# Four reorderings in a two-layer hybrid decoder step: scaled keys, held weight sums, split sample states, modulation panels in pairs

## The reference, cut to what matters

```
mod = silu(c) @ ada_w[l] + ada_b[l]            # 1024 x 9216, nine chunks of 1024
u   = rmsnorm(x) * (1 + sc1) + sh1
x   = x + 0.5 * g1 * swiglu(u, up, down)       # first FFN, 2816 hidden
proj = u @ w_in                                # four branches
y_b = rwkv7(...)                               # recurrence over tokens
merged = sum_i sigmoid(u @ w_gate[i]) * (y_i @ w_branch[i])
x   = x + g2 * (merged @ w_out)
x   = x + 0.5 * g3 * swiglu(u, up, down)       # second FFN
```

```
S = S * w_t + (S @ -kk_t) (kk_t * a_t)^T + v_t k_t^T ;  y_t = S @ r_t
```

## Time and profile before

| | us |
|---|---|
| median of 3 runs | 3047.55 |
| lowest, highest | 3044.19, 3050.33 |
| the profiled execution | 3045.21 |
| its span, first to last instruction | 3043.5 |

### The profile page before, as it was taken

One profiled execution on the slowest core, in us unless ns is written; L12 is line 12 of the kernel. 1 busy time (PEld: TensorE's weight loads), 2 busy tenths in 40 slices (PEclk: granted clock), 3 DMA queues, 4 the chain that ended last, 5 costly groups with the idle time before them and its releaser, 6 DMA issues.

```text
span 3043.5 us, 48463 instructions
## 1 busy us (share of the span) xinstructions
PE 3001.7 (99%) x19566; PEld 2461.5 (81%) x19566; DVE 1428.1 (47%) x3125; ACT 410.6 (13%) x782; POOL 1473.8 (48%) x1527
## 2 busy tenths in 40 slices
PE   8999999999999999999999999999999999999999
PEld 5889888677777878898878898876777778789987
DVE  4446522464344464565244564324544444555642
ACT  2000002202111120000010000022021111200000
POOL 4879530212120338896368894302222113599943
PEclk9999999999999999999999999999999999999999
DMA  6543223541111334222246322334311114122221
GB/s 262 216 165 111 101 99 132 171 139 41 53 54 61 117 115 167 98 84 91 76 173 229 125 84 86 126 122 153 129 59 53 53 60 159 70 84 84 84 87 68
DMA packets 73535, 337.81 MB, mean 111 GB/s; under 512 B 10592, under 2 KB 27744, under 8 KB 40288
## 3 DMA queue, kind: packets, MB, share of 16 engines
q1 hardware_dynamic: 63936, 312.03, 28.8%
q0 software_dynamic: 6816, 18.88, 2.1%
q10 hardware_dynamic: 2560, 3.80, 0.4%
HBM read 326.55 MB, written 6.02 MB: 109 GB/s over the span
## 4 chain that ended last, share of the span: by engine, by line
PE 91%; DVE 3%; POOL 3%; issue 1%; DMA 1%; ACT 1%; SPq 0%; POOLq 0%; DVEq 0%; ACTq 0%
PE ps L1000 90%; DVE ws L2287 1%; DMA y<-w_ada 1%; DVE u L2287 1%; DVE proj L2287 0%; POOL masked_room L901 0%; ACT ws L1966 0%; DVE y L2287 0%; POOL ws L860 0%; DVE masked_room L2287 0%; ACT u L1966 0%; POOL ws L866 0%; POOL ws L864 0%; POOL ws L868 0%; POOL ws L863 0%
## 5 line engine op out<-in xcount | busy, mean ns | idle before, releaser
L2287 DVE TENSOR_TENSOR ws<-ws,ps 128x272 f32<-128x272 f32 (+4 forms) x1650 | 620.2, 401 | 1122.2 <-PE ps L1000 1094.8
L1000 PE MATMUL ps<-u,ring 128*128 128x272 f32 (+1 forms) x4448 | 1040.3, 385 | 6.9 <-ACT u L1966 2.5
L1000 PEld LDWEIGHTS ps<-u,ring 128*128 128x128 f32 x4448 | 802.6, 191 | 187.8 <-issue 22.5
L1000 PE MATMUL ps<-y,ws 128*128 128x272 f32 (+1 forms) x1616 | 343.3, 348 | 0.0
L1000 PEld LDWEIGHTS ps<-y,ws 128*128 128x128 f32 x1616 | 265.4, 190 | 36.5 <-DVE ws L2287 3.7
L1966 ACT ACTIVATE ws<-ws 128x272 f32<-128x272 f32 (+5 forms) x226 | 137.0, 623 | 1116.6 <-DVE ws L2287 1065.1
L1000 PE MATMUL ps<-y,ring 128*128 128x272 f32 (+1 forms) x1376 | 276.9, 341 | 2.1 <-POOL ws L868 2.1
L846 POOL TENSOR_TENSOR masked_room<-ring 128x512 f32<-128x512 f32 (+1 forms) x36 | 46.7, 1297 | 424.4 <-PE ps L1000 170.8
L1000 PEld LDWEIGHTS ps<-y,ring 128*128 128x128 f32 x1376 | 219.0, 190 | 32.2 <-POOL ws L868 2.9
L1966 ACT ACTIVATE ws<-ps 128x272 f32<-128x272 f32 (+1 forms) x270 | 102.5, 395 | 861.3 <-PE ps L1000 861.2
L1000 PE MATMUL ps<-proj,ring 128*128 128x272 f32 x832 | 200.3, 393 | 1.5 <-DVE proj L2287 1.5
(11 more groups left out here) (249 smaller groups left out, 3825.4 us busy)
## 6 DMA issues: line engine op xcount, KB each, us to landing
ring<-w_up SPq DMA_DIRECT2D x88, 1024.0 KB, 4.9
proj<-w_ada SPq DMA_DIRECT2D x45, 1024.0 KB, 6.9
ring<-w_down SPq DMA_DIRECT2D x32, 1024.0 KB, 4.8
ring<-w_gate SPq DMA_DIRECT2D x32, 1024.0 KB, 4.9
ws<-w_ada SPq DMA_DIRECT2D x26, 1024.0 KB, 4.9
ring<-w_in SPq DMA_DIRECT2D x22, 1024.0 KB, 4.9
ws<-cache SPq DMA_DIRECT2D x128, 128.0 KB, 3.1
ws<-cache POOLq DMA_DIRECT2D x128, 128.0 KB, 3.4
```

The source lines that it names most:

```text
L1000: return nc.tensor.matmul(out, lhsT, rhs, start=start, stop=stop, skip_group_check=skip)
L2287: return V.tensor_tensor(out, a, b, op)
```

## The change

Four edits; no matmul, vector operation or transfer is added or removed.

1. `scaled` is cut in two. `scaled_keys` (Bt, Kt, Bp, Kp) of tile tt+1 is issued in tile tt, in the loop over chunks at ch = 0, behind the product `stmp`. `states_ahead` (`stmp` from v, `pend`, At, Rt, then the count of step 1) of tile tt+1 is issued at the end of tile tt, behind the copy of `yb`. `split_sum_12` of the second unit comes right behind it; before, it stood behind the next tile's `scaled`. For the samples it stands ahead of `scaled_states` and `scaled_keys` now.
2. `split_weight_sums(g)` on GpSimd waits, from unit 3 on, for a TensorE step: units 3, 5, 7, 9 for step 5 of the tile in which they are used, units 4, 6, 8 for step 12 of the tile before.
3. The sample state products are done in two halves of 32 records: the first between the fifth and sixth matmul of `fill(40)`, behind a new wait for VectorE's "c12" of unit 9, the second where all of them stood.
4. `side_modulation` for panel 0 moves behind `seven_[0]()`, beside panel 1; that for panel 2 moves to the end of the pair, beside panel 3.

```diff
                 def split_weight_sums(g):
+                    before, second = divmod(g - SPLIT[0] - 1, 2)
+                    if g > SPLIT[0]:
+                        pool.wait_ge(rw_pe.sem, rw_pe.upto(l, RW_PE * before + (12 if second else 5)))
                     s = panel_wait(pool, l, "gate", 2 * g)
...
                     two[0]()
-                    side_modulation(l, f, r, 0)
                     six[1]()
                     five(0)
                     two[1]()
...
                     seven_[0]()
+                    side_modulation(l, f, r, 0)
                     side_modulation(l, f, r, 1)
                     five(1)
                     seven_[1]()
...
                     four[0]()
-                    side_modulation(l, f, r, 2)
                     pair_sums(pe_, l, f, r, "S4a")
...
                     plain(5, raw(1, 4, 0), tok(4, HALF), False, part)
+                    side_modulation(l, f, r, 2)
                     side_modulation(l, f, r, 3)
...
-                fill(40)
+                fill(40, 0, 5)
+                split_dve(pe_, l, SPLIT[1] - 1, "c12")
+                sample_states(0)
+                fill(40, 5, 10)
                 pe_.wait_ge(rs_dve.sem, rs_dve.upto(l, 2))
                 pe_.wait_ge(rs_act.sem, rs_act.upto(l, 1))
                 settled(6)
                 m = small_heads(0, MA, MB)
+                sample_states(1)
...
-            def scaled(l, c, n, ends, split):
+            def scaled_states(c, n, ends):
                 V.tensor_copy(*ends)
                 stt(At[:, :, 0:n], kkv[:, :, c], -1.0, e2[:, :, c], MUL, MUL)
-                tt_(Rt[:, :, 0:n], r_[:, :, c], e1[:, :, c], MUL)
+                return tt_(Rt[:, :, 0:n], r_[:, :, c], e1[:, :, c], MUL)
+
+            def scaled_keys(l, c, n, ends, k):
                 tt_(Bt[:, :, 0:n], bv[:, :, c], e3[:, :, c], MUL)
                 link(l, tt_(Kt_[:, :, 0:n], k_[:, :, c], e3[:, :, c], MUL))
...
+                    def states_ahead(tt):
+                        V.tensor_copy(chunk_first(stmp), v_[:, :, tokens(tt)].rearrange("p f (c n) -> p f c n", c=2))
+                        scaled_states(tokens(tt), P, (pend, chunk_ends(tt))).then_inc(rw_dve.sem, 1)
+
                     if tt == 0:
+                        scaled_keys(l, c, P, chunk_ends(0), 2)
+                        states_ahead(0)
                         merges(l, 6, 8)
-                    else:
-                        split_sum_12(l, g0 - 1)
...
                         tt_(stmp[:, :, :], sbd[:, :, :], over(pend[:, :, ch], P), MUL)
+                        if ch == 0 and tt + 1 < NTT:
+                            scaled_keys(l, tokens(tt + 1), P, chunk_ends(tt + 1), 2)
...
                     V.tensor_copy(yb[:, :, c], ps[:, 2:4, 0:P]).then_inc(rw_dve.sem, 1)
+                    if tt + 1 < NTT:
+                        states_ahead(tt + 1)
+                    split_sum_12(l, g0 + 1)
...
-                scaled(l, slice(TP, T), TS, (pends, ends), NSEQ).then_inc(rs_dve.sem, 1)
-                split_sum_12(l, SPLIT[1] - 1)
+                scaled_states(slice(TP, T), TS, (pends, ends))
+                scaled_keys(l, slice(TP, T), TS, ends, NSEQ).then_inc(rs_dve.sem, 1)
```

More of the change, by code:

```diff
@@ L1887, in _, with sample_states @@
                 m.then_inc(rs_pe.sem, 1)
-                fill(40)
[L1889 to L1892, removed]
                 states = ps[:, 7, 0:4 * TS].rearrange("p (a f n) -> p a f n", a=2, f=2)
-                for ft in range(2):
+                def sample_states(ft):
                     for s in range(NSEQ):
@@ L1900, in _ @@
                                ARt[own, :, ft, s * TD:s * TD + TD], start=ft == 0 and s == 0, stop=False, skip=True)
+                fill(40, 0, 5)
+                split_dve(pe_, l, SPLIT[1] - 1, "c12")
+                sample_states(0)
+                fill(40, 5, 10)
+                pe_.wait_ge(rs_dve.sem, rs_dve.upto(l, 2))
+                pe_.wait_ge(rs_act.sem, rs_act.upto(l, 1))
+                settled(6)
+                m = small_heads(0, MA, MB)
+                sample_states(1)
                 for h in range(NH):
@@ L2895, in chunk_first @@
                 return v.rearrange("p c (f n) -> p f c n", f=2)
-            def scaled(l, c, n, ends, split):
+            def scaled_states(c, n, ends):
                 V.tensor_copy(*ends)
                 stt(At[:, :, 0:n], kkv[:, :, c], -1.0, e2[:, :, c], MUL, MUL)
-                tt_(Rt[:, :, 0:n], r_[:, :, c], e1[:, :, c], MUL)
+                return tt_(Rt[:, :, 0:n], r_[:, :, c], e1[:, :, c], MUL)
+            def scaled_keys(l, c, n, ends, k):
                 tt_(Bt[:, :, 0:n], bv[:, :, c], e3[:, :, c], MUL)
                 link(l, tt_(Kt_[:, :, 0:n], k_[:, :, c], e3[:, :, c], MUL))
-                e, k = ends[0], split
                 for o, i in ((Bp, Bt), (Kp, Kt_)):
@@ L2907, in scaled @@
                             i[:, :, 0:n].rearrange("p f (c n) -> p f c n", c=k),
-                            e.unsqueeze(3).to_broadcast([P, 2, k, n // k]), MUL)
+                            ends.unsqueeze(3).to_broadcast([P, 2, k, n // k]), MUL)
                 return m
@@ L2931, in added, with tokens, chunk_ends @@
                         return tt_(by_chunks(to), by_chunks(v), got, ADD)
[L2933 to L2936, removed]
+                    def tokens(tt):
+                        return slice(tt * P, tt * P + P)
+                    def chunk_ends(tt):
+                        return e1[:, :, tokens(tt)].rearrange("p f (c n) -> p f c n", c=2)[:, :, :, CH - 1]
+                    def states_ahead(tt):
+                        V.tensor_copy(chunk_first(stmp), v_[:, :, tokens(tt)].rearrange("p f (c n) -> p f c n", c=2))
+                        scaled_states(tokens(tt), P, (pend, chunk_ends(tt))).then_inc(rw_dve.sem, 1)
+                    c = tokens(tt)
                     if tt == 0:
+                        scaled_keys(l, c, P, chunk_ends(0), 2)
+                        states_ahead(0)
                         merges(l, 6, 8)
-                    else:
-                        split_sum_12(l, g0 - 1)
                     tile_pe(1)
```

## The result

The changed kernel takes 3028.1 us (median of 6 runs, 3027.79 to 3028.24) against 3047.28 for the kernel before (6 runs, 3044.19 to 3053.19). The ratio is 0.9935, with a 95% interval of 0.9922 to 0.9948: 19 us faster. The forecast was 3029.4 with a range of 3023 to 3038, and the measured time lies inside that range. The single runs of the changed kernel lie within 0.45 us of each other, those of the kernel before within 9.0.

A forecast was written before the change was run, and what follows sets the result against it. TensorE, busy 3001.7 us of the span, was taken as the bound. Scaled operands 1.92, held sums 7.30, sample states 2.6 and panels 6.3 gave 18.1 us; subtracted from the 3047.55 median, 3029.4, range 3023 to 3038.

The forecast's parts named there:

- Scaled operands: Start of tiles 2 and 3, both layers: moving four key operations to mid-tile removes TensorE's 0.48 us wait, 1.92 in all.
- Held sums: Three recurrence tiles: holding GpSimd's additions stops them stretching VectorE's ME and ME1 from 0.62 to 2.75 us; gain 7.30.
- more collisions: Recurrence tiles: more than three GpSimd collisions in the median kernel would give up to 4 us more, 3025; no chance given.
- Only the keys' 0.48?: TensorE's wait for the scaled operands before tiles 2 and 3 of both layers, priced separately at 4 x 0.48 us.
- Sample states: Sample products: halving the short stretch avoids clock drops behind it, 3.2 us less 0.6 for shape changes, net 2.6.
- Panels: Pairs with modulation panels: two panels moved beside others save 0.63 us per pair, 6.3 over ten pairs.
- the row of four: Modulation panels in a row: one more costs 0.86 us, against 1.18 standing alone, 0.32 less.
- pair 1 of layer 1: Eleventh pair, in `up0`: moving panel 0 uncovers a 0.6 us TensorE wait for GpSimd's "7s4", so no gain.
- The wait did not move to mid-tile: Rival, mid-tile: keys beside GpSimd delay `sat` 1.1 us in six tiles, 6.6; gain 11.5, 3036.0; chance 0.05.
- The side panels were never late: Rival, panel 1 of eight pairs: late loads make TensorE wait 5.3 us each; +38, 3085; chance 0.03.
- its cover: Mid-tile: 1.4 us of idle VectorE time behind the second `stmp` hides its delay by GpSimd, at most 1.3 us.

The follow-up runs named there:

- the last experiment: Changed kernel with side panel 0 back in its old place in pair 1 of `up0`, layer 1, and sample states in one piece after the small heads: 3027.18 us.

## Why the prediction was right, and which terms were off

*Scaled operands*, 1.92: measured 1.8 with the hold present. The four operations lie in mid-tile at no price, as argued.

*Held sums*, 7.30: right for the execution it was read from. The tiles gave back 9.23 against 1.92 + 7.30. It is the term that was too small for the median: alone on the kernel before the hold is worth 11.0, and on the changed kernel with the keys at the tile's end 3038.2 - 3029.6 = 8.6. The weak step is the choice of yardstick: the gain of one profiled execution was subtracted from the median, 2.3 above it, as if what lay between them were of another origin. The hold alone takes most of the spread away, so a good part of it was the collisions. They hang on the landing of a transfer (the releaser in brackets, twice above), so each execution can have its own; that the slower executions of the kernel before had more or dearer ones was not traced. The working itself had the sum for one execution, 3045.2 - 18.1 = 3027.1, 0.7 under the profiled one of the changed kernel. The rival of "more collisions" was on the right side with its up to 4 us more (3.7 by the medians), but it had no chance of its own and no place in the sum.

*Only the keys' 0.48?* Not without the hold. There their removal is worth 3038.2 - 3031.7 = 6.5 in the medians. The traces show one way in which the two parts work on one thing, the unit that starts half a microsecond later against the tile; how much of the 6.5 it makes is open. It was not foreseen: each part was given a price of its own.

*Sample states*, 2.6 net: the profiled pair of executions gave 2.71 (drops of 1.69 and 1.48 gone, less 0.31 and 0.15 for the cut where 0.3 each was taken). But the reason given, that the length of the short work brings the fall, did not hold: one piece of 2.04 us ran without a fall in the profiled runs of three other kernels, and in the one with the hold alone the two drops are gone with the piece uncut. So it is not shown that this edit gained anything. The edit's share in the median is 0.3 by the run with one piece and nothing by the last experiment. By what is left over elsewhere it is more: with the hold 3036.34 - 3027.80 - 1.8 - 5.1 = 1.6, without it 3047.29 - 3038.20 - 5.1 = 4.0, where the single runs of the two kernels spread over 12.1 and 9.9 us. The Trainium skill ("TensorE: Matmul & The Clock Gate", Part 1: The HAM clock gate (the "warmup" mystery)) says of the change from the lower level to the higher one that its point varies from run to run. For a fall the profiled runs of different kernels show something alike (2.56 in one, 4.25 in another behind the same 64 records); the two layers of one execution, which the prediction named as agreeing, can't show it. What sets it in an execution is open, and so is the value of this edit.

*Panels*, 6.3: measured 5.5 in the trace and 5.1 by the run. The size per pair was 0.56 and not 0.63: a panel that joins one other saves 0.28, where the row of four gave 0.32 for each. And pair 1 of layer 1 was given nothing, and lost 0.22; putting one panel back there is worth 0.6 in the median. The wait itself, with its place and its cause, was as argued (0.51 for the 0.6).

*The rivals.* The wait did not move to mid-tile: `sat` is released by TensorE, with 1.53 of idle time to spare. In the run without the hold the keys did take 4.6 us there beside GpSimd, and TensorE just missed waiting (47.19 for the tile), so this rival was near. The side panels were never late in the pairs; TensorE's one long wait for such a panel, 12.7 us at the start of the program, was there before (13.2). The Trainium skill ("SBUF — State Buffer", Who interferes with whom) would have the second `stmp` blocked by GpSimd in mid-tile: the trace agrees, 1.11 for 0.42, and its cover held.

In sum 1.8 + 11.0 + 5.1 + 1.6 = 19.5 us against the 19.2 measured and the 18.1 forecast. This sum is no check: its last term is the remainder that makes it come out. What it does show is that the forecast came so close partly by luck. The held sums were 3.7 too small for the median; the panels were 1.2 and the sample states at least 1.0 too large, and these errors stand against each other.

## What to carry to other kernels

When single runs of a kernel spread by several microseconds, look for work whose start is set by a transfer's landing and beside which operations of the critical chain take longer; tie its start to a step of the bounding engine. Here both the median and the spread fell. Don't subtract the gain read in one profiled execution from the median, when what is removed is what makes executions differ: the new kernel has no such distance between them (3027.79 and 3028.1). And where a sum comes out right, look at the terms: two of them were off in opposite directions here. Short operations of another array shape belong next to each other, but look at the sum that was covered by the one taken away.

## What the runs showed that was not expected

- The clock: 64 records of 8 columns, 2.04 us long, have ten records at the low level behind them in one kernel's execution (4.25 us) and at the full level in those of three others (2.56). A wait of 1.95 us, also ahead of small products, was followed by the full clock, one of 2.23 by the low one.
- Beside a GpSimd addition of 128x512 the sums ME and ME1, both inputs in SBUF, went from 0.31 us each to 1.38, an addition of 128x272 from 0.44 to 1.20, and a 128x256 copy from PSUM stayed at 0.41.
- Two edits that take away 1.8 and 3.9 us where the other one stays take away 10.4 together. A wait of 0.48 us that goes also moves a transfer's landing against the tile, and in the eight collisions traced half a microsecond is the difference between a wait of 1.2 and one of 2.0.
